# Expert weights by one queue, half of the combining on TensorE, and another order of the readout's loads

## The reference

```python
def expert_block(args):
    tok, e = args
    return swiglu(h_pad[tok], w_gate[e], w_up[e], w_down[e])       # (silu(h @ wg) * (h @ wu)) @ wd
...
weighted = (out.reshape(n_slots, d) * slot_w[:, None]).astype(h.dtype)
routed = jnp.zeros((t + 1, d), h.dtype).at[slot_tok].add(weighted)[:t]
return (routed + swiglu(hf, s_gate, s_up, s_down)).reshape(bsz, n, d)
...
def rwkv_readout(y, prep, r_k, lnx_g, lnx_b, w_out):
    yf = y[0] + jnp.flip(y[1], 1)                                   # then normalised per head, plus bonus
    ...
    o = (yn + bonus.reshape(B, T, D)) * jax.nn.silu(gate)
    return o @ w_out
```

## Time and profile before

| | |
|---|---|
| median of 3 executions | 2868.86 us (2866.93 to 2870.2) |
| the profiled execution's own time | 2869.81 us |
| its span | 2868.0 us |
| PE busy | 2465.2 us, 86% of the span |
| DVE busy | 1346.4 us, 47% |
| DMA moved | 471.24 MB, 164 GB/s on average |
| the experts' passes | about 794 to 1360 us of the span |
| the combining | 1373 to 1430 us |
| the readout | 2242 to about 2375 us |

### The profile page before, as it was taken

One profiled execution on the slowest core, in us unless ns is written; L12 is line 12 of the kernel. 1 busy time (PEld: TensorE's weight loads), 2 busy tenths in 40 slices (PEclk: granted clock), 3 DMA queues, 4 the chain that ended last, 5 costly groups with the idle time before them and its releaser, 6 DMA issues. The chain is left out here.

```text
span 2868.0 us, 45580 instructions
## 1 busy us (share of the span) xinstructions
PE 2465.2 (86%) x18102; PEld 1445.2 (50%) x18102; DVE 1346.4 (47%) x2688; ACT 709.0 (25%) x1273; POOL 487.4 (17%) x474
## 2 busy tenths in 40 slices
PE   4999764987899999998079999979999599989998
PEld 2554354954444443343035557448887346455553
DVE  1550646533611111111678895976666561044442
ACT  3111440102211111111225561123333113044441
POOL 0000142300111111111000000033332230035550
PEclk7999776999899999999589999999999799999999
DMA  6110610014789999996525656334554832021001
GB/s 243 67 59 1 235 23 17 7 59 168 268 333 391 387 418 407 399 388 262 204 87 136 169 153 191 114 121 131 136 164 124 319 118 97 8 42 22 10 30 66
DMA packets 328951, 471.24 MB, mean 164 GB/s; under 512 B 151497, under 2 KB 225139, under 8 KB 304037
## 3 DMA queue, kind: packets, MB, share of 16 engines
q1 hardware_dynamic: 302677, 373.92, 37.9%
q10 hardware_dynamic: 12960, 69.21, 5.9%
q0 software_dynamic: 13104, 25.19, 2.3%
HBM read 413.82 MB, written 76.55 MB: 171 GB/s over the span
## 5 line engine op out<-in xcount | busy, mean ns | idle before, releaser
L1980 PE MATMUL psum<-ex_w,hT 128*64 128x512 f32 (+1 forms) x1104 | 330.6, 619 | 27.4 <-DMA ex_w<-in_exp_w_up 25.7
L1980 PEld LDWEIGHTS psum<-ex_w,hT 128*64 128x64 f32 (+1 forms) x1104 | 125.6, 159 | 226.7 <-issue 224.4
L4126 POOL TENSOR_SCALAR mla_pool<-mla_pool,at_stats 128x768 f32<-128x768 f32 x64 | 140.3, 2206 | 253.1 <-DVE at_stats L4144 253.1
L2212 DVE COPY slot_act_t<-psum 128x256 f32<-128x256 f32 x45 | 19.1, 424 | 327.0 <-PE psum L1988 327.0
L551 PE MATMUL psum<-hT,weights 128*128 128x512 f32 x384 | 166.8, 592 | 0.0
L1996 PE MATMUL psum<-ex_w,slot_act_t 128*64 128x512 f32 (+1 forms) x552 | 163.4, 597 | 1.4 <-DVE slot_act_t L2212 1.4
L1965 POOL DMA_INDIRECT scratch_ys<-slot_out,slot_row x45 | 45.4, 1008 | 468.2 <-issue 405.6
L551 PEld LDWEIGHTS psum<-hT,weights 128*128 128x128 f32 x384 | 73.0, 190 | 86.7 <-issue 86.1
L2168 ACT ACTIVATE slot_silu<-psum 128x256 f32<-128x256 f32 x45 | 17.3, 385 | 400.2 <-PE psum L1980 400.2
L3323 PE MATMUL psum<-rs_r_ident,rs_k_ident 64*64 64x96 f32 x1536 | 86.5, 252 | 15.3 <-POOL rs_k_ident L3295 14.0
L4024 PE MATMUL psum<-mla_kT,at_qT 128*128 128x512 f32 (+1 forms) x256 | 93.3, 489 | 2.6 <-DVE at_qT L4136 1.6
(11 more groups left out here) (612 smaller groups left out, 4731.0 us busy)
## 6 DMA issues: line engine op xcount, KB each, us to landing
ex_w<-in_exp_w_gate SPq DMA_DIRECT2D x64, 1024.0 KB, 9.1
ex_w<-in_exp_w_up SPq DMA_DIRECT2D x64, 1024.0 KB, 18.9
ex_w<-in_exp_w_down ACTq DMA_DIRECT2D x60, 1024.0 KB, 10.2
mod_ring<-in_w_mod SPq DMA_DIRECT2D x12, 2048.0 KB, 14.0
scratch_features<-tokens SPq DMA_DIRECT2D x96, 256.0 KB, 3.7
weights<-in_w_in SPq DMA_DIRECT2D x6, 2048.0 KB, 8.0
ex_w<-in_mod_w SPq DMA_DIRECT2D x6, 2048.0 KB, 12.5
ex_w<-scratch_ys SPq DMA_DIRECT2D x8, 1536.0 KB, 19.0
```

Source lines behind the costliest of these rows:

```text
L1980: mm = pe.matmul(bank[at:at + n, :], XT[:, k, at:at + n], W[:, 0:2, k * DE:(k + 1) * DE], start=(k == 0), stop=(k == KD - 1))
L4126: pool.tensor_scalar(Pm[:, q % 2, u, :], Pm[:, q % 2, u, :], st[:, 3, u:u + 1], None, ALU.mult)\
```

## The change

Three edits. First, SP requests all three matrices of an expert, in the order gate, up, down; the wait for `down_done` now stands on SP between up and down, and ACT requests none:

```diff
                 sp.wait_ge(S["up_done"], last_pass(q - AT_ONCE) + 1)
                 load_expert(sp, Wb, buffer_of(q), e, gu[buffer_of(q)], (0, 1))
+                sp.wait_ge(S["down_done"], 2 * (last_pass(q - AT_ONCE) + 1))
+                load_expert(sp, Wb, buffer_of(q), e, dn[buffer_of(q)], (2,))
...
-                for q in range(AT_ONCE, NE):
-                    if last_pass(q - AT_ONCE) == t:
-                        e = src(expert_at(act, order, q))
-                        act.wait_ge(S["down_done"], 2 * (t + 1))
-                        load_expert(act, Wb, buffer_of(q), e, dn[buffer_of(q)], (2,))
```

Second, in tiles 1 to 3 of the combining, the last three of the six weighted rows are summed on PE, as products with diagonal matrices that ACT makes ahead of its other work; DVE adds the sum from PSUM. Two squares of ACT are moved ahead of the last tile:

```diff
+            for j in range(1, JX):
+                pe.wait_ge(S["diag_set"], HALF * j)
+                pe.wait_ge(S[f"in{LOADS.index((j, 1))}"], 16)
+                if j > 2:
+                    pe.wait_ge(S["added"], TOP_K + (j - 2) * (HALF + 1))
+                for n in range(2):
+                    for m in range(HALF):
+                        mm = pe.matmul(total(j)[:, n * 512:(n + 1) * 512], diag[:, j - 1, m, :],
+                                       rows[:, j, HALF + m, n * 512:(n + 1) * 512], start=(m == 0), stop=(m == HALF - 1))
+                mm.then_inc(S["half_mm"], 1)
...
+            for j in range(1, JX):
+                for m in range(HALF):
+                    act.activation(diag[:, j - 1, m, :], K.ident, ACT.Copy, scale=w_of[:, HALF + m, j:j + 1])\
+                        .then_inc(S["diag_set"], 1)
             for j in range(JX):
                 lengths(j)
                 if j:
                     next_lengths(j - 1)
-            act.wait_ge(S["ctx_in"], 16)
-            for j in range(JC):
-                square(K.X[:, j, :], st[:, 3, j:j + 1], squares[0])
+                if j == JX - 2:
+                    act.wait_ge(S["ctx_in"], 16)
+                    for n in range(JC):
+                        square(K.X[:, n, :], st[:, 3, n:n + 1], squares[0])
             next_lengths(JX - 1)
...
+                if j:
+                    dve.wait_ge(S["half_mm"], j)
+                    dve.wait_ge(S["added"], done + HALF)
+                    dve.tensor_tensor(acc[:, j, :], acc[:, j, :], total(j), ALU.add).then_inc(S["added"], 1)
```

Third, SP's order in the readout:

```diff
             vectors_in(sp, I, vec, S["vec_in"])
+            for b in range(2):
+                sp.wait_ge(S[f"y_st{b}"], 16 * 4 * 2 * NT)
+            sp.wait_ge(S["turned"], 1)
+            R.load(sp, 2)
             M.load(sp, 0)
...
             M.load(sp, 1)
-            M.load(sp, 2)
...
-            for j in range(2, NT):
+            for j in range(3, NT):
                 sp.wait_ge(S["turned"], j - 1)
                 R.load(sp, j)
-                if j < 5:
-                    M.load(sp, j + 1)
+                M.load(sp, j - 1)
+            M.load(sp, NT - 1)
```

More of the change, by code:

```diff
@@ L2370, in combine @@
     LOADS = [(j, h) for j in range(JX) for h in range(2)]
-    names = ("added gated ctx_in g_in sq_done rms_done v_step normed rms2_done " + " ".join(f"in{n}" for n in range(len(LOADS))))
+    names = ("diag_set half_mm added gated ctx_in g_in sq_done rms_done v_step normed rms2_done " + " ".join(f"in{n}" for n in range(len(LOADS))))
     with ExitStack() as c, phase(nc, names) as (block, S):
@@ L2375, in combine, with _ @@
         rows = spare[:, 0:JX * TOP_K * D].rearrange("p (j k n) -> p j k n", j=JX, k=TOP_K)
+        HALF = TOP_K // 2
+        diag = buf("weight_diagonals", [P, JX - 1, HALF, P])
+        total = lambda j: K.psum[:, (j % 2) * 2 * 512:(j % 2 + 1) * 2 * 512]
+        @block.tensor
+        def _(pe):
+            for j in range(1, JX):
[8 more added lines that the diff above has]
+                mm.then_inc(S["half_mm"], 1)
         @block.sync
@@ L2431, in _ @@
             for j in range(JX):
-                for k in range(TOP_K):
-                    if k % (TOP_K // 2) == 0:
-                        dve.wait_ge(S[f"in{LOADS.index((j, k // (TOP_K // 2)))}"], 16)
+                done = TOP_K + (j - 1) * (HALF + 1) if j else 0
+                for k in range(HALF if j else TOP_K):
+                    if k % HALF == 0:
+                        dve.wait_ge(S[f"in{LOADS.index((j, k // HALF))}"], 16)
                     if k:
-                        dve.wait_ge(S["added"], j * TOP_K + k)
+                        dve.wait_ge(S["added"], done + k)
                     dve.scalar_tensor_tensor(out=acc[:, j, :], in0=rows[:, j, k, :], scalar=w_of[:, k, j:j + 1],
                                              in1=acc[:, j, :], op0=ALU.mult, op1=ALU.add).then_inc(S["added"], 1)
-                dve.wait_ge(S["added"], (j + 1) * TOP_K)
+                if j:
+                    dve.wait_ge(S["half_mm"], j)
+                    dve.wait_ge(S["added"], done + HALF)
+                    dve.tensor_tensor(acc[:, j, :], acc[:, j, :], total(j), ALU.add).then_inc(S["added"], 1)
+                dve.wait_ge(S["added"], TOP_K + j * (HALF + 1))
                 dve.tensor_tensor(acc[:, j, :], acc[:, j, :], gate, ALU.mult).then_inc(S["gated"], 1)
@@ L3568, in _ @@
             M.load(sp, 1)
-            M.load(sp, 2)
-            for b in range(2):
-                sp.wait_ge(S[f"y_st{b}"], 16 * 4 * 2 * NT)
-            for j in range(2, NT):
+            for j in range(3, NT):
                 sp.wait_ge(S["turned"], j - 1)
                 R.load(sp, j)
-                if j < 5:
-                    M.load(sp, j + 1)
+                M.load(sp, j - 1)
+            M.load(sp, NT - 1)
             sp.wait_ge(S["x_in"], 48)
```

## The result

The changed kernel takes 2888.74 us (median of 6 executions, 2881.22 to 2894.47); the kernel before took 2869.07 beside it. The ratio is 1.0067, 95% interval [1.0051, 1.0084]: slower by 19.7 us where 7 were forecast, and inside the stated range.

| stretch | before | after | difference |
|---|---|---|---|
| to `up(0)` | 792.1 | 792.9 | +0.8 |
| experts, `up(0)` to the last `up` | 558.1 | 589.2 | +31.0 |
| to the combining's first addition | 29.1 | 29.0 | -0.1 |
| combining, to `token_inv` on DVE | 51.0 | 47.8 | -3.2 |
| stages between (not edited) | 811.8 | 805.7 | -6.1 |

The account below looks back on a forecast made before the run. DMA was taken to bound the experts' paired passes, DVE the combining, neither DVE nor PE the readout's beginning. 2869.8 + 17.3 - 5.1 - 5.1 = 2876.9, 0.95 off for the median: 2876 us; 8-in-10 range 2858 to 2898.

Parts of the forecast that it names:

- the first dry stretch: Experts' stage: DMA queues empty from 809.74 to 818.6, 8.9 us, while SP waits until 815.78 to request expert 4's down.
- the rhythm of the waits: Experts, from pass 18 on: a wait of 5.0 with slow products (2.1), then one of 0.1, 7.2 lost in four passes.
- The start: Experts up to pass 16: 2.1 of wait at `up(5)` plus 1.0 of short waits, together 3.1 us lost.
- Wait: 2.1: `up(5)`: wants expert 8's up at 850.70, which was forecast to land at 852.8, so PE waits 2.1 us.
- The few late landings behind it: Experts up to pass 16: requests landing in 11.8 against 11.78 us, a few waits of up to 0.5, together 1.0.
- The pairs: Experts from pass 16 on, 14 pairs of passes loading three experts each: 50.3 us lost, where 36.1 was lost before.
- Four products of 512 columns took 3.75: Combining, PE: the rate at clock 0.52 from which six products were forecast to take 5.6 us.
- The combining: Combining: DVE does fewer additions, tile 1 2.0 late, 3.2 gained by tile 3, squares 1.9: -5.1 us, from -2 to -9.
- The readout: Readout's beginning: tile 2's arrays requested ahead of tokens and gate rows, `norm(2)` at 2270.5 instead of 2275.61: -5.1 us, from 0 to -7.
- hidden: Rival, experts' weights: same bytes and rate, SP's waits end before the queue is dry, 0 us, total 2859; chance 0.15.
- The order pays: Rival, experts' weights: gate and up no longer share engines with another expert's down, -18 us, total 2841; chance 0.09.
- Dry in every pair: Rival, experts' pairs of passes: SP reaches the next request too late, queue dry each time, +38 us, total 2897; chance 0.21.

## Why the prediction came out as it did

The direction was right, and so were the first dry stretch and the rhythm of the waits. But the loss was nearly three times the forecast one: the weights cost 31.0 in this kernel, where the sum had 17.3, and 6.1 us that nobody had forecast took a part of it back. Without these, by chance of the right sign, the time would be about 2895, near the range's end.

- **The start, 3.1 predicted, 12.6 by pass 17.** The dry stretch was forecast at 8.9 us and came with 8.7. The failed step is "Wait: 2.1", with "only 3.1 of it and what follows reaches PE" behind it, and ahead of it the landing of expert 8's up, 843.94 + 8.9. That added the dry time to a landing of the kernel before, in which down of expert 7 did not stand ahead in the same line; up landed at 856.9 in place of 852.8. Pass 5 waited 5.38, and its products lost 2.9 more, which the term did not have. The run with that down moved shows its share of the wait (6.2 to 3.06). The price was in the prediction's own first paragraph, where letting the queues run dry costs its whole length: by pass 17 the edit with the dry start lost some 9 us more than the edit without it. The few late landings behind it, 1.0 predicted, came to about 3.
- **The pairs, 14.2 predicted (50.3 less 36.1), about 18 measured.** From pass 18 on, waits and slow products sum to 54.0 us, in the predicted rhythm; the second wait is 0.8 to 1.9, not 0.1, and the loss by slow products 1.9 on average, not 2.1. What makes the waits is right only in part. The queues dry for 2.75 us in every second pair would be 5% of the time; the busy share fell by 2 points, while the rate fell by 5%. Why the engines moved less while they were busy is open.
- **The combining, -5.1 predicted, -3.2 measured.** "Four products of 512 columns took 3.75" was misread: the four rows are two products, since each counts twice. At that rate six take 11; in tile 1 they took 7.9, not 5.6, since the clock, which the sum left at 0.52, rose to 1.00 after about 5 us. So tile 1 is 4.2 late, not 2.0. The rest held: tiles 2 and 3 gain 2.7 each without waiting, the squares 2.0.
- **The readout, -5.1 predicted, -4.6 measured.** PE's transposes of tile 2 come 4.8 earlier from the stage's start, 42.4 against 47.2. The gate rows are 4.75 later (5.6 predicted). DVE's first addition takes 3.56 in place of 1.23, so its reduction behind it gains only 3.9.
- **Not predicted: 6.1 us between.** 3.7 of it lies in the part in which PE's idle time moved; the other 2.4 are within what the rest of the stretch varies by.

The rivals: "hidden" is what happens with one queue in the order of the waits' ends (a stage of 555.2 us, 558.1 before), and not with this one. "The order pays" is refuted by the same run. "Dry in every pair" would have been +38; the weights' edit alone comes to 37 to 40, but not in that way: long and short waits alternate, and over a third of the stage's loss falls ahead of the pairs.

## What to carry to other kernels

Merging the request queues cost no bandwidth here; the waits that came with the requests cost 37 to 40 us. Write each request where its wait ends. In a stage that DMA bounds, price a change by the time in which the engines stand dry (8.7 us dry, some 9 lost by pass 17), and not by the first instruction that waits.

Work given to an idle engine has to be counted in that engine's own rows: see first how many rows one call makes, and at which granted clock the engine runs them.

## What the runs showed of the hardware

PE stood idle for about 3.3 us with no releaser in the profile, then ran at a granted clock of 0.71 for 5.8 us, some 110 us behind the combining. The row of the kernel before:

```profile
1540.19 0.53 PE L2731 MATMUL psum<-tokens 64*32 64x32 f32 x37 [3.32 <-issue]
```

It stands there in all seven runs without products in the combining (3.15 to 3.32 us) and in none of the six with 24 or 36 more rows on PE ahead of it, used or not. The trace shows what else went on in it. The DMA view of 1536.9 to 1540.1 us has one packet of the queue that the page calls `instruction`, 16 KB:

```profile
q8 instruction: 1, 0.02, 1.8%
```

It ends 1.4 us before PE goes on. This is so each time: between 105 and 475 us behind the combining the 13 traces have 42 idle times of PE of 1.5 us or more without a releaser, and in every one PE goes on 1.2 to 1.6 us after the end of such a packet. Most of these packets, 17 or 18 of 20 or 21 in that stretch of a run, come with no such idle time. So PE most likely waits there for its own instructions, and rows added ahead move the places where it has to. No run tested this.

The idle time of 1.8 to 2.3 us ahead of tile 3's sums, in the five runs with 36 rows, is another matter: it ends about 0.1 us after the last of the eight loads has landed, and costs nothing there. In the run whose sums are not used the profile names that load:

```profile
1405.83 7.07 PE L2388 MATMUL psum<-ex_w,weight_diagonals 128*128 128x512 f32 x12 [2.28 <-DMA ex_w<-scratch_ys]
```
